# A hybrid decoder step: sample logits turned behind mix unit 2, query norm split, values a unit sooner, gate quarters one a step

## What is computed

```
x  = x + 0.5 * swiglu_ffn(rms_norm(x), w_ffn1_in, w_ffn1_out)          # 1024 -> 2816 -> 1024
h  = rms_norm(x)
a, b, q, k, v, qi, ki, wi, gc, ga = split(h @ w_in)                     # one input projection
u  = a * sigmoid(b); q, k = rope(rms_norm(q)), rope(rms_norm(k)); gates = sigmoid(gc), sigmoid(ga)
conv = silu(layer_norm(depthwise_conv31(u))) @ w_cout
idx  = top_k(sum_heads(wi * relu(qi . ki)), 256 per query, at most)     # sample: over 4096 cached keys
att  = softmax(q . K[idx] / 8) @ V[idx]                                 # sample: K, V gathered from paged caches
x  = x + (gate_c * conv + gate_a * (att @ w_aout)) @ w_o
x  = x + 0.5 * swiglu_ffn(rms_norm(x), w_ffn2_in, w_ffn2_out)
```

## Time and profile before

| what | value |
|---|---|
| median of three executions | 1489.83 us |
| the profiled execution's own time | 1490.01 us |
| its span in the trace | 1488.2 us |
| TensorE busy | 1424.3 us, 96% |
| VectorE busy | 1050.9 us, 71% |
| GpSimd busy | 592.2 us, 40% |
| ScalarE busy | 548.5 us, 37% |

### The profile page before, as it was taken

One profiled execution on the slowest core, in us unless ns is written; L12 is line 12 of the kernel. 1 busy time (PEld: TensorE's weight loads), 2 busy tenths in 40 slices (PEclk: granted clock), 3 DMA queues, 4 the chain that ended last, 5 costly groups with the idle time before them and its releaser, 6 DMA issues. The chain is left out here.

```text
span 1488.2 us, 20869 instructions
## 1 busy us (share of the span) xinstructions
PE 1424.3 (96%) x8219; PEld 1117.0 (75%) x8219; DVE 1050.9 (71%) x1685; ACT 548.5 (37%) x841; POOL 592.2 (40%) x414
## 2 busy tenths in 40 slices
PE   5989999999999999999999899999998999999998
PEld 2224678777888876436766566689998999999998
DVE  1356788989746899998997998567689765674221
ACT  3134655325712331122112234443374444452111
POOL 2000565444369846552345777132305455320000
PEclk9999999999999999999999999999999999999999
DMA  9995363232267878867458777332421322312222
GB/s 339 364 387 206 98 87 109 85 100 71 72 199 238 289 251 304 283 213 246 142 165 281 263 222 234 126 121 86 137 76 57 114 86 86 114 51 71 83 88 85
DMA packets 155874, 246.66 MB, mean 166 GB/s; under 512 B 11901, under 2 KB 104845, under 8 KB 155515
## 3 DMA queue, kind: packets, MB, share of 16 engines
q1 hardware_dynamic: 130734, 162.26, 33.4%
q0 software_dynamic: 23056, 76.03, 16.2%
q10 hardware_dynamic: 1989, 7.07, 1.2%
HBM read 235.48 MB, written 10.20 MB: 165 GB/s over the span
## 5 line engine op out<-in xcount | busy, mean ns | idle before, releaser
L2826 POOL TENSOR_TENSOR w_lo<-w_raw,w_hi 128x1024 fp32r<-128x1024 f32 x65 | 172.2, 2650 | 224.8 <-ACT w_hi L1352 224.6
L698 PE MATMUL ps<-bh,wqr 128*128 128x288 f32 x936 | 205.4, 295 | 4.2 <-DVE wqr L1969 1.9
L2896 POOL DMA_INDIRECT kv<-cache_v,idxT x128 | 138.0, 1078 | 96.9 <-PE ps L1130 48.8
L1352 ACT ACTIVATE w_hi<-w_raw 128x1024 fp32r<-128x1024 f32 (+1 forms) x88 | 91.3, 1037 | 225.2 <-PE ps L649 178.0
L2884 POOL DMA_INDIRECT kv<-cache_k,idxT x128 | 138.8, 1085 | 83.9 <-DVE kprod L2517 51.8
L698 PEld LDWEIGHTS ps<-bh,wqr 128*128 128x128 f32 x936 | 155.6, 188 | 5.0 <-DVE wqr L1969 3.8
L649 PE MATMUL ps<-h_hi,w_hi 128*128 128x512 f32 x352 | 138.9, 395 | 2.1 <-POOL w_lo L2826 2.1
L649 PE MATMUL ps<-h_hi,w_lo 128*128 128x512 f32 x352 | 137.3, 390 | 0.0
L649 PE MATMUL ps<-h_lo,w_hi 128*128 128x512 f32 x352 | 137.1, 390 | 0.0
L714 PE MATMUL ps<-a_hi,wqr 128*128 128x288 f32 x704 | 122.4, 295 | 0.0
L698 PE MATMUL ps<-bl,wqr 128*128 128x288 f32 x384 | 113.4, 295 | 0.0
(11 more groups left out here) (522 smaller groups left out, 3174.3 us busy)
## 6 DMA issues: line engine op xcount, KB each, us to landing
w_raw<-w_ffn_in SPq DMA_DIRECT2D x56, 512.0 KB, 3.7
wq<-w_ffn_in SPq DMA_DIRECT2D x40, 512.0 KB, 3.5
wn<-w_in SPq DMA_DIRECT2D x36, 512.0 KB, 6.2
qb<-q_scratch SPq DMA_DIRECT2D x64, 256.0 KB, 5.3
ring<-w_ffn_in SPq DMA_DIRECT2D x28, 512.0 KB, 11.1
w_raw<-w_ffn_out SPq DMA_DIRECT2D x24, 512.0 KB, 3.4
wq<-w_ffn_out SPq DMA_DIRECT2D x20, 512.0 KB, 3.4
ring<-w_ffn_out SPq DMA_DIRECT2D x14, 512.0 KB, 11.0
```

Source lines behind the costliest of these rows:

```text
L698: mm = pe.matmul(ps[:, bank + m, 0:HALF], w[:, k, m * P:(m + 1) * P], b[:, j, k, :], start=(j in (0, 1, 5) and k == 0 and fst), stop=(k == ...
L1352: act.activation(w_hi[:, slot, 0:n], w_raw[:, slot, 0:n], ACT.Copy).then_inc(S_("hi_ready"), 1)
L2826: pool.tensor_tensor(w_lo[:, slot, 0:n], w_raw[:, slot, 0:n], w_hi[:, slot, 0:n].bitcast(F32), ALU.subtract)\
L2896: pool.indirect_dma_start(kv[:, V_SLOT[j % 3] + a // 2, a % 2, :], None, rows[1], bass.IndirectOffsetOnAxis(ap=idxT[:, j % 2, t:t + 1], ax ...
```

## The change

- `mix_sums` moves behind k-step 3 of column group 0 instead of k-step 2.
- The wait for the relus at the head of group 3 is split: row block b waits for `prelu_ready` 21 + b.
- `logits_turn` moves from behind mix unit 3 to behind unit 2 and writes banks 0 to 3 instead of 4 to 7; it waits for the first sigmoid (`mix_free` 1), no longer for `u_ready` 2, which `probs_turn` now waits for. Unit 4 waits until VectorE has emptied those banks.
- The sample values that stand between mix units come one unit sooner (batches 10 and 11 at the end), `fill(2)` of their operand on ScalarE two gates sooner.
- On VectorE `prompt_qk` is split into mean, scale and rope; seven rounds of choice and the logits' block go behind the mean, `u_pair(0)` behind them, scale before the sum block and rope after it. `own_heads(0)` goes ahead of `choose(3)`.
- The last gate group's quarters are spread one to a step over steps 12 to 15, instead of two each in steps 12 and 13.
- The first gather of index keys waits for `ring_used` 60 instead of 64, and `turn_ik` of it comes behind column group 1 instead of group 0.

```diff
--- before.py
+++ after.py
@@ -329,10 +329,10 @@
 
         PAIR = ("ping_free", "pong_free")
         N_MIX = 14
-        V_AFTER = {7: (0, 1), 9: (2,), 10: (4,), 11: (6,), 13: (9, 10)}
-        V_WITHIN = {10: 3, 11: 5, 12: 7, 13: 8}
-        QUARTERS = ((0, 1), (2,), (3,), (4, 5), (6,), (7,), (8, 9), (10,), (11,), (12, 13), (14,), (15,), (16, 17), (18, 19))
-        VALUES = ((11, 12), (13,), (14, 15), (16,), (17, 18), (19,), (20, 21), (22,), (23,), (24, 25), (26, 27), (28,), (29, 30), (31,))
+        V_AFTER = {6: (0, 1), 8: (2,), 9: (4,), 10: (6,), 12: (9,), 13: (10, 11)}
+        V_WITHIN = {9: 3, 10: 5, 11: 7, 12: 8}
+        QUARTERS = ((0, 1), (2,), (3,), (4, 5), (6,), (7,), (8, 9), (10,), (11,), (12, 13), (14,), (15,), (16,), (17,), (18,), (19,))
+        VALUES = ((12,), (13,), (14, 15), (16,), (17, 18), (19,), (20, 21), (22,), (23,), (24, 25), (26, 27), (28,), (29, 30), (31,))
         FILL_AT = {j - 1: n // 2 for j, ns in enumerate(VALUES) for n in ns if n % 2 == 0 and n >= 14}
         HEADS_AT = {j + 1: n // 8 for j, ns in enumerate(VALUES) for n in ns if n % 8 == 7}
         V_SLOT, V_SEM, V_KEYS = (4, 0, 2), (4, 5, 0), (60, 62, 64)
@@ -845,9 +845,9 @@
                     stream_mm(g, 2, n, hTs, 2 * j, j == 0, j == 3)
                 if g == 0:
                     turn_h(1, 3)
+                if g == 1:
                     turn_ik(0, 0)
                     turn_ik(0, 4)
-                if g == 1:
                     pe.wait_ge(S_("iro_ready"), 1)
                     for j in range(3):
                         mm = pe.transpose(ps[:, 4, j * NS:(j + 1) * NS], iros[:, 0, 4 * j:4 * j + 4, :].rearrange("p a b -> p (a b)"), ident[0:NS, 0:NS])
@@ -1056,8 +1056,6 @@
             pe.wait_ge(S_("idxT_ready"), 1)
             for g, n in enumerate((NI, DA, DA, DA)):
                 for j in range(4):
-                    if g == 3 and j == 0:
-                        pe.wait_ge(S_("prelu_ready"), 24)
                     if g == 0:
                         pe.wait_ge(S_("xg_ready"), 2 * j + 2)
                     if g == 1 and j == 0:
@@ -1070,6 +1068,8 @@
                         s = 4 * g + b
                         if j == 0 and s >= 8:
                             pe.wait_ge(S_("nat_evac"), s - 7)
+                        if g == 3 and j == 0:
+                            pe.wait_ge(S_("prelu_ready"), 21 + b)
                         if j == 0 and s == 2:
                             pe.wait_ge(S_("pong_free"), taken[1])
                         for k in range(2):
@@ -1080,7 +1080,7 @@
                     if g == 3 and j < 3:
                         mm = sample_values(j, wt)
                     mm.then_inc(S_("ring_used"), 1)
-                    if g == 0 and j == 2:
+                    if g == 0 and j == 3:
                         mix_sums()
                     if g == 2:
                         if j == 0:
@@ -1097,7 +1097,7 @@
                 if n == 2:
                     pe.wait_ge(S_("nat_evac"), 16)
                 if n == 4:
-                    pe.wait_ge(S_("mix_free"), 1)
+                    pe.wait_ge(S_("logitsT_evac"), 1)
                 if n == 6:
                     pe.wait_ge(S_("mix_free"), 2)
                 if n == 8:
@@ -1143,15 +1143,16 @@
             def logits_turn():
 
                 pe.wait_ge(S_("logits_ready"), NS + 1)
-                pe.wait_ge(S_("u_ready"), 2)
+                pe.wait_ge(S_("mix_free"), 1)
                 for h in range(H):
                     for c in range(2):
-                        mm = pe.transpose(ps[0:NS, 4 + h // 2, (h % 2) * 256 + c * P:(h % 2) * 256 + (c + 1) * P], G[:, c * H + h, :], ident[:, :])
+                        mm = pe.transpose(ps[0:NS, h // 2, (h % 2) * 256 + c * P:(h % 2) * 256 + (c + 1) * P], G[:, c * H + h, :], ident[:, :])
                 mm.then_inc(S_("logitsT_done"), 1)
 
             def probs_turn():
 
                 pe.wait_ge(S_("shift_ready"), 2)
+                pe.wait_ge(S_("u_ready"), 2)
                 for c in range(2):
                     for h in range(H):
                         pe.transpose(ps[:, 5 + c, h * NS:(h + 1) * NS], L[:, h, c * P:(c + 1) * P], ident[0:NS, 0:NS])
@@ -1206,7 +1207,7 @@
                         qk_turn(2 if n == 12 else 6)
 
                 mix_unit(n, between)
-                if n == 3:
+                if n == 2:
                     logits_turn()
                 if n == 5:
                     probs_turn()
@@ -1739,6 +1740,7 @@
             act.wait_ge(S_("zq_zero"), 2)
             fill(0)
             fill(1)
+            fill(2)
             act.wait_ge(S_("u_ready"), 4)
             act.activation(gpack[:, :, :].rearrange("p k (s t) -> p k s t", s=NSEQ), U_s[:, :, :, CW - 1:CW - 1 + NEW], ACT.Copy).then_inc(S_("us_state"), 1)
             qk_root(1)
@@ -1785,7 +1787,6 @@
                 sigmoid(0, ACT.Tanh, 0.5)
                 save_gate(i)
                 if i == 0:
-                    fill(2)
                     fill(3)
                     state_evac()
                 if i == 1:
@@ -2610,17 +2611,26 @@
 
             msq = small[:, 8:8 + 4 * H]
 
-            def prompt_qk(w):
-
-                src, g = ((qn, gqb), (kn, gkb))[w]
+            def qk_mean(w):
+
+                src = (qn, kn)[w]
                 dve.wait_ge(S_("nat_evac"), 4 * (w + 2))
                 v = src[:, :, :].rearrange("p b (h d) -> p (b h) d", d=HD)
                 qk_squares(v, rt1[:, :, :, :].rearrange("p b h d -> p (b h) d"), msq, rt2[:, 0, 0:1, :].rearrange("p a b -> p (a b)"))\
                     .then_inc(S_("ms_ready"), 1)
+
+            def qk_scale(w):
+
+                src, g = ((qn, gqb), (kn, gkb))[w]
+                v = src[:, :, :].rearrange("p b (h d) -> p (b h) d", d=HD)
                 dve.wait_ge(S_("root_ready"), ROOT["qk"[w]])
                 lk(dve.reciprocal(msq, msq))
                 lk(dve.tensor_tensor(v, v, msq.unsqueeze(2).to_broadcast([P, 4 * H, HD]), ALU.mult))
                 lk(dve.tensor_tensor(v, v, g[:, :].unsqueeze(1).to_broadcast([P, 4 * H, HD]), ALU.mult))
+
+            def qk_rope(w):
+
+                src = (qn, kn)[w]
                 v4 = src[:, :, :].rearrange("p b (h two d) -> p b h two d", two=2, d=32)
                 cs = [ropetp[:, 1:TB, c:c + 32].unsqueeze(2).to_broadcast([P, 4, H, 32]) for c in (0, 32)]
                 rope(v4[:, :, :, 0, :], v4[:, :, :, 1, :], v4[:, :, :, 0, :], v4[:, :, :, 1, :], cs[0], cs[1], rt1[:, :, :, :], rt2[:, :, :, :])
@@ -2629,31 +2639,34 @@
             late = keys_at(UA + 12, UM + NATIVE)
             for n in late:
                 key_logits(n)
-            prompt_qk(0)
-            dve.wait_ge(S_("ring_used"), N_RING + NB)
-            link(dve.memset(U_p[:, :, 0:CW - 1], 0.0))
-            u_pair(0)
-            choose(1, 0, 2)
+            qk_mean(0)
+            choose(1, 0, 7)
             dve.wait_ge(S_("logitsT_done"), 1)
             link(dve.tensor_copy(L[:, :, TOPK_S:TOPK_S + NS], nlog[:, :, :]))
-            dve.tensor_tensor(L[:, :, 0:TOPK_S], ps[0:NS, 4:8, :].rearrange("p b (h n) -> p (b h) n", h=2),
+            dve.tensor_tensor(L[:, :, 0:TOPK_S], ps[0:NS, 0:4, :].rearrange("p b (h n) -> p (b h) n", h=2),
                               slotbias[:, :].unsqueeze(1).to_broadcast([NS, H, TOPK_S]), ALU.add).then_inc(S_("logitsT_evac"), 1)
             dve.wait_ge(S_("logitsT_evac"), 1)
             settle()
             mx, sm = small[0:NS, 40:48], small[0:NS, 50:58]
             lk(dve.tensor_reduce(mx, L[:, :, :], AX.X, ALU.max))
             dve.tensor_tensor(L[:, :, :], L[:, :, :], mx.unsqueeze(2).to_broadcast([NS, H, TOPK_S + NS]), ALU.subtract).then_inc(S_("shift_ready"), 1)
-            choose(1, 2, 5)
+            dve.wait_ge(S_("ring_used"), N_RING + NB)
+            link(dve.memset(U_p[:, :, 0:CW - 1], 0.0))
+            u_pair(0)
+            qk_scale(0)
             dve.wait_ge(S_("exp_ready"), 1)
             lk(dve.tensor_reduce(sm, L[:, :, :], AX.X, ALU.add))
             lk(dve.reciprocal(sm, sm))
             dve.tensor_tensor(L[:, :, :], L[:, :, :], sm.unsqueeze(2).to_broadcast([NS, H, TOPK_S + NS]), ALU.mult).then_inc(S_("shift_ready"), 1)
-            choose(1, 5, 16)
+            qk_rope(0)
+            choose(1, 7, 16)
             choose(2, 0, 5)
             u_pair(1)
             dve.wait_ge(S_("ssq_ready"), 4)
             link(dve.tensor_tensor(vns[:, :], vns[:, :], vpart[:, :], ALU.add))
-            prompt_qk(1)
+            qk_mean(1)
+            qk_scale(1)
+            qk_rope(1)
 
             def prompt_mask(b, n, t):
 
@@ -2680,9 +2693,8 @@
                 dve.tensor_tensor((mz if g < 2 else mzb)[:, g % 2, :], ps[:, 4, :], headmask[:, :], ALU.mult).then_inc(S_("mz_ready"), 1)
 
             choose(2, 5, 16)
-            choose(3, 0, 2)
             own_heads(0)
-            choose(3, 2, 16)
+            choose(3, 0, 16)
 
             ys = yacc[:, :, 0:NS].rearrange("p k (s t) -> p k s t", s=NSEQ)
```

(2 more changed lines are left out.)

## The result

The changed kernel took 1502.09 us (median of four, 1501.42 to 1505.23) against 1490.63 us for the kernel before beside it: ratio 1.0086, 95% interval 1.0066 to 1.0105, so 11.5 us. Forecast were 1498.5 us and a range of 1488 to 1503.5. The profiled execution of the changed kernel was the longest of its four, 1505.23 us with a span of 1503.4 us; its trace accounts for 15.2 us of span, nearly 4 us more than the medians show.

What follows compares the result with a forecast made beforehand. TensorE, busy 96% of the span in one fixed order, was taken to bound the kernel. 1490.0 + 3.6 + 6.3 + 1.2 - 2.4 gave 1498.7 us, 1498.5 us as median; range 1488 to 1503.5 us.

Steps and rivals of the forecast that it cites:

- E: Stage behind the attention, to the end: no change forecast, 0 us.
- A: First index gather four loads sooner, 97 to 131 us: it delays the last `w_ffn1_out` load, +3.6 us.
- B: Prompt projection, 557 to 693 us: sums moved behind k-step 3 uncover its tile's landing, +6.3 us.
- C: Mix units, 683 to 818 us: old waits go, a new pause at unit 8 takes the gain back, +1.2 us.
- the 12% share: Index gather stretch: the gather in full flow holds the engines 92% and leaves the weight streams 12%.
- rival 1: Index gather shares evenly (+1.2 us there, 1496.1 us total) or hurts nobody (-1.2 us, 1493.7 us); chance 0.19.
- low clock: TensorE at 1.2 instead of 2.4 GHz after some pauses: +1.8 us in B, +1.1 us at unit 8 in C.
- D: Attention steps, 818 to 966 us: the sample-value wait goes, VectorE's masks limit the gain, -2.4 us.
- VectorE's queue: Mix units: VectorE's new order ends `u_pair(1)` at 755.3 us, TensorE arrives at 751.5, so unit 8 waits 3.9 us.
- rival 2: Prompt projection: k-step 3's tile lands in time without the sums, B = 0, 1492.2 us; chance 0.12.
- rival 3: Moved transfers find slack and land in time, no new pauses or low clock: 1482.3 us; chance 0.10.
- Rival 4: Everything moved is paid back in place, A and B are mild: 1490 us; chance 0.12.

Runs made afterwards that it cites:

- the gather's own run: Kernel before with only the first index gather at `ring_used` 60 and its transposes behind column group 1: 1492.12 us, ratio 1.002.
- gather at 62: Kernel before with the first index gather at `ring_used` 62 and its transposes behind column group 1: 1489.71 us, ratio 0.9996.
- the sums' own run: Kernel before with only `mix_sums` moved behind k-step 3; the table's "sums alone": 1497.84 us, ratio 1.0072.
- the kernel without sums and gather: Changed kernel with `mix_sums` back behind k-step 2, gather back at 64, `turn_ik` back behind group 0: 1488.98 us, ratio 1.0004.
- the new quarters alone: Kernel before with only the last gate group's quarters one a step; the table's "quarters alone": 1489.76 us, ratio 0.9996.
- the first two runs: Kernel before with only `mix_sums` moved behind k-step 3 (1497.84 us), and with only the gather at 60, transposes behind group 1 (1492.12 us).
- the kernel with the values back: Changed kernel, sums and gather undone, `u_pair(1)` ahead of `choose(2, 0, 5)`, values 0 and 1 back behind unit 7: 1482.97 us, ratio 0.9953.
- relus' wait whole: Best kernel (1480.82 us) with `prelu_ready` 24 ahead of group 3 again, the wait unsplit: 1484.87 us, ratio 0.9957.
- best with old quarters: Best kernel (1480.82 us) with the old quarters, two in steps 12 and 13: 1483.18 us, ratio 0.9944.

## Why the prediction was right, point by point

The median lies 3.6 us above the forecast and 1.4 us inside the range. The terms do less well against the profile: they sum to 8.7 us where its span grew by 15.2. E, for which nothing was forecast, is the largest part of the gap, and the median is nearer because the profiled execution was the longest of four. So the nearness of the total is in part luck; the pauses of A, B and C that carry it came where they were forecast.

**A, right in mechanism, slightly high** (+3.6; +2.9 in the changed kernel, +3.1 in the gather's own run). The step that the 12% share would shut out the last load is what the rows show: 4.56 us of waits for the last two loads. (A slip in the sum did no harm: 2.1 MB at 0.385 MB/us are 5.5 us, not 5.6, which gives the +4.8 that was taken.) Two things were not foreseen. The load before the last waits too. And after the pause TensorE stayed at the lower clock up to 118 us. The half share of rival 1 did not come: it forecast 2.4 us later for the last load, and the two waits sum to nearly twice that. The turns are equal in packets, 48 and 48, but not in bytes, 0.79 against 0.07 MB. The gathers at 62 and at 64 fit a stretch that is bounded by bytes: with the keys' wait gone, a weight tile waits 1.5 or 2.2 us.

**B, right in mechanism, low by 1.5 us** (+6.3; +7.8). Pause 5.43 us (forecast 5.1), means in the open 0.98, group 1 at +6.7 from the start of group 0 (590.02 - 559.2 = 30.8 against 24.1; forecast +5.5). VectorE's wait at L2559 was 12.9 us (forecast 11). The mis-sized term is low clock, on both sides. K-step 3 took 7.05 instead of 5.92 us, and group 1 37.66 us where the same 80 matmuls took 34.57: 4.2 us together for a forecast of +1.8. Against this, with the relus' pause the low clock behind it went too (the first 16 matmuls of group 3 took 7.13 us for 8.83), 1.7 us that the forecast hadn't counted (not in every kernel with the split: the same 16 took 8.57 us in the one without sums and gather). VectorE's lateness cost under 1 us here; the relus' wait of 4.10 us in the sums' own run shows what it costs when that wait isn't split. The two rows of the kernel before:

```profile
580.93 34.57 PE L1077 MATMUL ps<-wn,xg 128*128 128x512 f32 x80 [0.79 <-DMA wn<-w_in]
...
649.50 8.83 PE L1077 MATMUL ps<-wn,xg 128*128 128x512 f32 x16 [1.27 <-ACT rp L1688]
```

**C, one step failed** (+1.2; +3.6). The pause at unit 8 came as forecast (3.61 for 3.9), and so did unit 12's (0.41 for 0.5). Three things were off. First, value batch 11 now lies ahead of step 0: 1.0 us that belongs to D. Second, low clock behind the pause cost 10.74 - 7.9 = 2.8 us where +1.1 was taken (9.72 us for the unit, or 1.8, behind the pause of 3.50 us in the kernel without sums and gather). The busy time by stretch in the changed kernel (us, PE, PEld, DVE, ACT, POOL, then granted clock, DMA share, GB/s):

```profile
764.00:766.00 2.00, 1.21 (x3) 0.93 (x4) 1.97 (x5) 1.22 (x2) 0.00 (x0) 0.50 0.75 277
766.00:768.00 2.00, 2.00 (x6) 1.43 (x5) 1.93 (x3) 0.48 (x1) 0.00 (x0) 0.50 0.01 2
768.00:770.00 2.00, 2.00 (x6) 1.43 (x5) 1.97 (x2) 0.00 (x0) 0.00 (x0) 0.50 0.00 0
```

The clock is at half already when unit 8 begins and for all 6 us shown; behind the logits' pause the mean of 0.72 over 6 us makes about 3.4 us at half clock. Third, the reason given for the pause was "VectorE's queue", and the runs show this for about one half of it; the other 1.87 us are a cover that was lost, the same mistake of the change as in B. The forecast had the right pause from both (it took values 0 and 1 out of TensorE's side), but named one cause.

**D, right in sum, but not told from chance** (-2.4; -2.3, of which 1.0 is value batch 11). With the attention steps as before, the wait for gathered values alone was 1.9 to 4.35 us and D 144.7 to 148.1 us, so one pair of profiles can't show 2 us. The wait for the gathered values is gone from its old place; `plogits` of steps 6 and 9 wait 0.64 and 0.96 us for VectorE's masks, as forecast for step 9, and a later batch waits 1.20 us.

**E, not foreseen** (0; +3.8). In the eight kernels with the changed VectorE order E takes 524.3 to 525.8 us; in the six with the old order 522.1 to 524.5. What divides them in the traces is a pause at L604 for `w_lo` with low clock behind it. In the nine kernels over 524 us the pause is 1.84 to 2.60 us and half clock follows it for 3.4 us; in the other five it is 1.29 to 1.83 us and none follows there. The two groups nearly touch, so that the pause's length alone decides isn't shown. In the changed kernel the pause is 0.85 us longer and the half clock costs at most 1.7 us; a microsecond or so of the +3.8 isn't assigned. How the pause gets its length is shown below. It hangs on how far GpSimd starts ahead of VectorE there: 0.68 to 1.36 us with the old order (1.07 with the new quarters alone), 0.81 with the new order and the old quarters, and between 0.44 us ahead and 0.30 us behind with both. Why, stays open.

The chances had 0.49 on slower by over 0.5%, and that is what was measured. Rivals 1 and 2 fell by the first two runs, rival 3 with them. Rival 4 is nearly the kernel without sums and gather (1488.98 us): there the wait for `u_pair(0)` that C removes is paid back at unit 8.

The best kernel (`u_pair(1)` first, values 0 and 1 behind unit 7, sums and the gather's start as before, the rest of the change kept) takes 1480.82 us, 0.5% under the kernel before and 1.4% under the changed one.

## What to carry to other kernels

Work that looks like a filler on the busiest engine may be the cover of a load or of another engine's step: before moving it, look at what lands or ends at its end, to the tenth of a microsecond. When a wait is removed by reordering an engine's queue, write out the new queue to the next point where the first engine needs it, and put the needed step first, not behind filler rounds. A bulk gather sent early into a saturated DMA stream takes its time from the loads that are under way when its data flow: at 60 these were the last two of the FFN, at 62 none of them.

## What the hardware showed that was not expected

VectorE's `w_lo` split (1.2 us alone) and GpSimd's first product of the second FFN (2.4 us alone) exclude each other. Whichever starts first finishes at its own pace, and the other stands until then. In the changed kernel, GpSimd then VectorE:

```profile
1066.22 2.42 POOL L2973 TENSOR_TENSOR wq<-wq 128x1024 f32<-128x1024 f32 x1 [29.70 <-DMA wq<-w_ffn_in]
```

```profile
1066.27 3.45 DVE L1939 TENSOR_TENSOR w_lo<-w_raw,w_hi 128x1024 fp32r<-128x1024 f32 x1
```

and in the kernel with the values back, where VectorE is first by 0.02 us:

```profile
1044.06 3.46 POOL L2973 TENSOR_TENSOR wq<-wq 128x1024 f32<-128x1024 f32 x1 [29.76 <-DMA wq<-w_ffn_in]
```

```profile
1044.04 1.22 DVE L1939 TENSOR_TENSOR w_lo<-w_raw,w_hi 128x1024 fp32r<-128x1024 f32 x1
```

| kernel | VectorE starts after GpSimd by | VectorE's duration | sum | pause of TensorE at L604 |
|---|---|---|---|---|
| changed | 0.05 | 3.45 | 3.50 | 2.60 |
| relus' wait whole | 0.44 | 3.04 | 3.48 | 2.20 |
| best with old quarters | 0.81 | 2.69 | 3.50 | 1.84 |
| before | 0.90 | 2.60 | 3.50 | 1.75 |
| quarters alone | 1.07 | 2.42 | 3.49 | 1.57 |
| gather at 62 | 1.32 | 2.18 | 3.50 | 1.35 |
| sums alone | 1.36 | 2.13 | 3.49 | 1.29 |

In all seven VectorE ends 3.5 us after GpSimd's start, that is 1.1 us after GpSimd's end, while GpSimd keeps its 2.40 to 2.42 us however much the two overlap: VectorE was not slowed, it waited. (The other four kernels with GpSimd first give 3.48 to 3.51.) The Trainium skill (SBUF — State Buffer, section "SBUF: two separate sides") calls the port pair that VectorE and GpSimd share an exclusive lock, held for a whole instruction, not a shared bandwidth; these rows agree with it. In each row the start and the pause of TensorE add up to 2.64 to 2.67 us: each tenth of a microsecond by which GpSimd starts less far ahead lengthens the pause by a tenth. In the three kernels where VectorE is first the pause is 2.44 to 2.45 us. So when the two engines meet decides up to 1.3 us of pause, and the low clock behind it up to 1.7 us more. The meeting differs from kernel to kernel also where nothing near it was changed, and moves the time by as much as the smaller parts of a change.

The second surprise was how large the low clock's share is. Of the 15.2 us of span in the changed kernel's profile, 5.4 are longer busy time for the same matmuls. Among them are 1.1 us in k-step 3, 3.1 in group 1 and 2.8 in unit 8, less what was saved elsewhere, as the 1.7 us in group 3.
